# Joining two consecutive gate or up pieces of an expert into one 2 MiB transfer in a fused attention, mLSTM and MoE layer

## The reference, cut to what matters

```python
hg = jnp.einsum('td,edf->tef', xt, w_gate)            # w_gate, w_up: 16 x 2048 x 512
hu = jnp.einsum('td,edf->tef', xt, w_up)
h = jax.nn.silu(hg) * hu * combine[:, :, None]
ff = jnp.einsum('tef,efd->td', h, w_down)             # w_down: 16 x 512 x 2048
ple = (p[l] @ w_ple[l]) * jax.nn.sigmoid(h1 @ w_ple_gate[l])   # w_ple_gate: 2048 x 2048
out = layer_norm(DN_ALPHA * h1 + ff + ple, ln2_g[l], ln2_b[l])
```

## Time and profile before

| | us |
|---|---|
| median of three runs | 1544.24 |
| the profiled execution, its own time | 1543.46 |
| its span, first to last instruction | 1541.9 |
| PE busy in the span | 1482.8 |
| DVE busy | 679.3 |
| ACT busy | 507.1 |
| expert matmuls, gate and up (L896), busy | 227.7 |
| expert matmuls, down (L936), busy | 99.6 |
| PLE gate chunks (L835), busy | 99.0 |

### The profile page before, as it was taken

One profiled execution on the slowest core, in us unless ns is written; L12 is line 12 of the kernel. 1 busy time (PEld: TensorE's weight loads), 2 busy tenths in 40 slices (PEclk: granted clock), 3 DMA queues, 4 the chain that ended last, 5 costly groups with the idle time before them and its releaser, 6 DMA issues.

```text
span 1541.9 us, 16783 instructions
## 1 busy us (share of the span) xinstructions
PE 1482.8 (96%) x6612; PEld 997.9 (65%) x6612; DVE 679.3 (44%) x932; ACT 507.1 (33%) x691; POOL 53.9 (3%) x62
## 2 busy tenths in 40 slices
PE   7999999999999999999999999899998999999893
PEld 6887788888777888888888886533433533343331
DVE  5546665457656555454545655611022121211136
ACT  4444444455544444434444433400200200020011
POOL 0000000043300000000000000000000000000000
PEclk9999999999999999999999999999999999999996
DMA  9554555554444555655555965099999999999994
GB/s 304 184 171 163 164 173 197 176 164 151 149 137 135 167 183 186 203 191 191 190 192 191 364 225 186 9 407 416 389 417 419 419 396 418 419 392 418 419 403 165
DMA packets 132205, 394.88 MB, mean 256 GB/s; under 512 B 13216, under 2 KB 15904, under 8 KB 107552
## 3 DMA queue, kind: packets, MB, share of 16 engines
q1 hardware_dynamic: 123552, 386.56, 67.6%
q10 hardware_dynamic: 8576, 7.28, 1.4%
HBM read 391.71 MB, written 2.10 MB: 255 GB/s over the span
## 4 chain that ended last, share of the span: by engine, by line
PE 61%; issue 37%; DVE 1%; DMA 1%; ACT 0%; SPq 0%; POOLq 0%; DVEq 0%; POOL 0%
PE bank L472 19%; PE bank L473 18%; PE bank L477 18%; PE bank L767 1%; PE bank L499 1%; PE bank L630 1%; PE bank L652 1%; DMA w_ring<-in_w_in_dram 1%; PE bank L564 1%; PE bank L643 0%; PE bank L679 0%; PE bank L678 0%; DVE res L2121 0%; DVE res L2127 0%; PE bank L737 0%
## 5 line engine op out<-in xcount | busy, mean ns | idle before, releaser
L1465 DVE TENSOR_TENSOR w_lo<-w_ring,w_hi 128x1024 fp32r<-128x1024 f32 (+1 forms) x312 | 381.8, 1226 | 307.3 <-ACT w_hi L1062 306.5
L1062 ACT ACTIVATE w_hi<-w_ring 128x1024 fp32r<-128x1024 f32 (+1 forms) x312 | 327.3, 1050 | 317.4 <-PE bank L477 313.7
L472 PE MATMUL bank<-w_hi,xT_hi 128*128 128x512 f32 (+1 forms) x864 | 346.5, 401 | 3.9 <-ACT w_hi L1062 3.9
L473 PE MATMUL bank<-w_hi,xT_lo 128*128 128x512 f32 (+1 forms) x864 | 334.9, 388 | 0.0
L896 PE MATMUL bank<-moe_ring,xg 128*64 128x512 f32 x1024 | 227.7, 595 | 14.3 <-DMA moe_ring<-in_w_up_dram 8.4
L477 PE MATMUL bank<-w_lo,xT_hi 128*128 128x512 f32 (+1 forms) x864 | 229.3, 387 | 0.0
L472 PEld LDWEIGHTS bank<-w_hi,xT_hi 128*128 128x128 f32 x864 | 162.3, 188 | 40.5 <-issue 7.6
L473 PEld LDWEIGHTS bank<-w_hi,xT_lo 128*128 128x128 f32 x864 | 162.5, 188 | 32.4 <-issue 1.9
L477 PEld LDWEIGHTS bank<-w_lo,xT_hi 128*128 128x128 f32 x864 | 161.6, 188 | 33.2
L896 PEld LDWEIGHTS bank<-moe_ring,xg 128*64 128x64 f32 x1024 | 73.9, 137 | 162.1 <-issue 160.7
L936 PE MATMUL bank<-moe_ring,moe_hiddenT 128*64 128x512 f32 x448 | 99.6, 594 | 2.0 <-DMA moe_ring<-in_w_down_dram 2.0
(11 more groups left out here) (272 smaller groups left out, 1343.0 us busy)
## 6 DMA issues: line engine op xcount, KB each, us to landing
w_ring<-in_w_in_dram SPq DMA_DIRECT2D x104, 1024.0 KB, 5.0
moe_ring<-in_w_gate_dram SPq DMA_DIRECT2D x64, 1024.0 KB, 11.9
moe_ring<-in_w_up_dram SPq DMA_DIRECT2D x64, 1024.0 KB, 12.8
moe_ring<-in_w_down_dram SPq DMA_DIRECT2D x64, 1024.0 KB, 12.7
w_ring<-in_w_proj_a_dram SPq DMA_DIRECT2D x16, 1024.0 KB, 5.0
w_ring<-in_w_proj_m_dram SPq DMA_DIRECT2D x16, 1024.0 KB, 5.0
w_ring<-in_w_out_dram SPq DMA_DIRECT2D x16, 1024.0 KB, 5.7
moe_ring<-in_w_ple_gate_dram SPq DMA_DIRECT2D x14, 1024.0 KB, 10.8
```

The costliest lines, as they stand in the source:

```text
L472: mm(b, lh(k, m), WH[:, s, kk, 0:width], start=start and kk == 0, stop=False)
L473: mm(b, ll(k, m), WH[:, s, kk, 0:width], start=False, stop=False)
L1062: fn(WH[:, h % 4, :, 0:width], W32[:, h // 2, 2 * (h % 2):2 * (h % 2) + 2, 0:width], ACT.Copy).then_inc(hi_ready, 1)
L1465: v.tensor_tensor(WL[:, h % 4, :, 0:width], W32[:, h // 2, 2 * (h % 2):2 * (h % 2) + 2, 0:width], WH[:, h % 4, :, 0:width].bitcast(F32), A ...
```

## The change

- The 8 up slots of a pair come in another order: `up_place(i)` gives gate groups 0 and 1, up groups 0 and 1, gate 2 and 3, up 2 and 3.
- The loads of two consecutive slots (always the same matrix) are listed as expert 0 of both, then expert 1 of both. Where their two places adjoin (not places 7 and 0), one transfer of 2 MiB loads both, with rows of 16 KB, and increments the semaphore of the first place alone. `LANDED` says for each piece which semaphore and which value tell that it is there.
- SP waits for such a transfer until both places are free.
- PE adds 4 to `ring_used` after every second up slot, in place of 2 after each.
- PLE chunks 0 and 2 stand behind slot 3 of pairs 0 and 1, not behind slot 2.
- ACT's sigmoid waits for slot 5 in place of slot 6.
- The overflow path (more than 64 tokens for an expert) keeps its single transfers, with its semaphore values adjusted. It does not run with these inputs.

```diff
@@ -62,7 +62,7 @@
-CHUNKS_IN = (("up", 0, 2), ("up", 0, 5), ("up", 1, 2), ("up", 1, 5), ("up", 2, 5), ("down", 1, 1), ("up", 3, 5),
+CHUNKS_IN = (("up", 0, 3), ("up", 0, 5), ("up", 1, 3), ("up", 1, 5), ("up", 2, 5), ("down", 1, 1), ("up", 3, 5),
@@ -74,12 +74,41 @@
     for slot in range(SLOTS_OF[item[0]]):
-        LOADS += [item + (slot, 0), item + (slot, 1)]
+        if item[0] == "down":
+            LOADS += [item + (slot, 0), item + (slot, 1)]
+        elif slot % 2:
+            LOADS += [item + (s, e) for e in range(2) for s in (slot - 1, slot)]
...
+def joint(m):
+
+    return LOADS[m][0] == "up" and LOADS[m][2] % 2 == 0 and m % RING < RING - 1
+
+SIGNALS = [0] * RING
+LANDED = []
+for m in range(N_LOADS):
+    if m and joint(m - 1):
+        LANDED.append(LANDED[-1])
+    else:
+        SIGNALS[m % RING] += 16
+        LANDED.append((m % RING, SIGNALS[m % RING]))
...
+def up_place(i):
+
+    return 2 * (i // 4) + i % 2, i // 2 % 2
@@ -334,23 +363,25 @@
-            def ring_load(m, dst, src):
+            def ring_load(m, dst, src, n=1):
 
+                s, m = m % RING, m + n - 1
                 if m < 4:
                     sp.wait_ge(lo_ready, HALVES * T_END + 2 * m + 2)
                 elif m < RING:
                     sp.wait_ge(slot_free, SLOT_CREDIT + HALVES * T_END)
                 else:
                     sp.wait_ge(ring_used, m - RING + 1)
-                sp.dma_start(dst, src).then_inc(ring_in[m % RING], 16)
+                sp.dma_start(dst, src).then_inc(ring_in[s], 16)
...
-                    ring_load(m, ring_rows(s), up_part(2 * n + e, i))
+                    if joint(m):
+                        ring_load(m, ring_rows(s, 2), up_part(2 * n + e, i, 2), 2)
+                    elif not m or not joint(m - 1):
+                        ring_load(m, ring_rows(s), up_part(2 * n + e, i))
@@ -821,7 +855,7 @@
-                pe.wait_ge(ring_in[m % RING], 16 * (m // RING + 1))
+                pe.wait_ge(ring_in[LANDED[m][0]], LANDED[m][1])
@@ -906,7 +940,9 @@
-                    up_slot(w, i, b, 2 * (n % 2)).then_inc(ring_used, 2)
+                    last = up_slot(w, i, b, 2 * (n % 2))
+                    if i % 2:
+                        last.then_inc(ring_used, 4)
@@ -1377,7 +1413,7 @@
             def sig(n):
-                used("up", n, UP_SLOTS - 2)
+                used("up", n, UP_SLOTS - 3)
```

More of the change, by code:

```diff
@@ L82, with landed_over_at @@
 PAIR_LOADS = 2 * (UP_SLOTS + DOWN_SLOTS)
+def joint(m):
[8 more added lines that the diff above has]
+        LANDED.append((m % RING, SIGNALS[m % RING]))
+def landed_over_at(m):
+    first = N_LOADS + (m - N_LOADS) % RING
+    return SIGNALS[m % RING] + 16 * ((m - first) // RING + 1)
+def up_place(i):
+    return 2 * (i // 4) + i % 2, i // 2 % 2
 def turn_bank(n):
@@ L335, in _, with up_part, ring_rows @@
             down_v = w_down.rearrange("l e (t p) n -> p (l e) t n", p=P)
[L337 to L343, removed]
-            def ring_load(m, dst, src):
+            def up_part(e0, i, n=1):
+                kg, mat = up_place(i)
+                w = up_v if mat else gate_v
+                return w[:, bass.ds(e0, 1), 4 * kg:4 * kg + 4 * n, :].rearrange("p e t f -> p (e t) f")
+            def ring_rows(s, n=1):
+                return RW[:, s:s + n, :].rearrange("p s (t f) -> p (s t) f", t=4)
+            def ring_load(m, dst, src, n=1):
+                s, m = m % RING, m + n - 1
                 if m < 4:
@@ L893, in up_slot @@
                 for t in range(4):
-                    k = 4 * (i // 2) + t
+                    k = 4 * up_place(i)[0] + t
                     for e in range(2):
-                        last = mm(B[b0 + i % 2][CAP * e:CAP * e + CAP, :], xg[:, k, (e0 + e) * CAP:(e0 + e) * CAP + CAP],
+                        last = mm(B[b0 + up_place(i)[1]][CAP * e:CAP * e + CAP, :], xg[:, k, (e0 + e) * CAP:(e0 + e) * CAP + CAP],
                                   w[e][:, t * NC:t * NC + NC], start=k == 0, stop=k == KT - 1)
@@ L1025, in landed_over @@
                                     m = m0 + 2 * i + e
-                                    pe.wait_ge(ring_in[m % RING], 16 * (m // RING + 1) + 16 * (2 * PAIR_LOADS // RING) * g)
+                                    pe.wait_ge(ring_in[m % RING], landed_over_at(m) + 16 * (2 * PAIR_LOADS // RING) * g)
                                 return [RW[:, (m0 + 2 * i + e) % RING, :] for e in range(2)]
```

## The result

| | before | changed |
|---|---|---|
| median, us | 1543.88 (4 runs, 1542.23 to 1544.55) | 1596.45 (4 runs, 1593.37 to 1600.33) |
| ratio, 95% interval | | 1.0343 (1.0328 to 1.0358) |
| profiled execution, span | 1541.9 | 1591.6 (own time 1593.37) |
| mean granted clock | 0.990 | 0.979 |

The change costs 52.6 us, twice the forecast of 26 and beyond the end of the range (1590). The direction and the place are as forecast; the size is not.

A forecast was written before the change was run, and what follows sets the result against it. The prediction took DMA and PE, nearly level over an eight-place ring, as the bound from about 1000 us. It added 25.7 us of PE waits to 1543.46, giving 1569.2, and 0.8 for the median: 1570 us, range 1556 to 1590.

The forecast's parts named there:

- What bounds the kernel: From about 1000 us, DMA (127.6 us per two pairs) and PE (124 us) are within 5%, eight ring places between them.
- The mechanism: Gate and up slots free four places after two slots and need both 2 MiB transfers landed, so PE waits and DMA runs dry.
- the walk: Place-by-place calculation of the expert part from traced durations: PE waits 15.3 us before the change, 41.0 us after.
- The rate of the 16 KB row: Gate and up loads: 2 MiB takes 4.93 us against 5.00, 4 us less transfer in all, bounds 0 and 7.
- carried on place by place: Expert part, transfers in queue order with traced durations: 25.7 us more PE waits than the kernel before.
- price of 2.05 us: SP's ring queue: time from a release of places until bytes flow, taken from the release at 999.8 us.
- slow long rows: 16 KB rows flow much slower, towards the instruction fetches' price: 1610 us at 3.0 us a MiB, beyond 1700 at full price; 5%.
- no difference: Dry spots mostly vanish or are hidden by PE's work, leaving 1552 us or less; 7%, of which 3% within 0.2%.
- a fixed cost for each transfer: Each queued transfer carries a fixed cost that merging halves, making the kernel faster, for example 1540 or 1532 us; 4%.
- The signs: Profile from 1000 us: gate and up waits about 39 us, 375 to 400 GB/s, 2 MiB landing median above 10 us.
- the clock rival: PE's clock falls after eight waits of about 3 us or more in the expert part, losing 23 us: 1593 us; 12%.
- The range: Eight-in-ten range for the whole kernel, 1556 to 1590 us, covering the forecast's own 1562 to 1583 and most of the clock case.

The follow-up runs named there:

- split rows: Changed kernel with each joined 2 MiB transfer issued as two of 1 MiB with 8 KB rows, back to back, same waits: 1598.97 us, ratio 1.0354.
- One place less: Kernel before the change, with SP waiting for one more freed place ahead of each load, as if the ring had 7 places: 1552.09 us, ratio 1.0056.
- the release by four: Kernel before with new slot order and moved PLE chunks, plus 4 places freed after every second up slot; 1 MiB transfers loaded slot by slot: 1554.70 us, ratio 1.0061.
- the expert order: Changed kernel with only the joining switched off: expert 0's two pieces, then expert 1's, 1 MiB each, 4 places freed together: 1567.87 us, ratio 1.0140.
- two places less: Kernel before the change, with SP waiting for two more freed places ahead of each load, as if the ring had 6 places: 1576.79 us, ratio 1.0219.
- the runs with idle matmuls: Changed kernel with identity matmuls on PE ahead of its waits, three amounts: full 1604.40 us, half 1583.52 us, half without those lacking a wait 1586.75 us.

## Why the prediction was wrong

- **What bounds the kernel** was right: the first 996 us did not change, and everything lies in the balance of DMA and PE over the ring.
- **The mechanism** was right: waits at the slots that the walk named, the first at 1016.5 us (forecast: near 1017), the ring's first load at 1002.6 (1003.6), the DMA dry in many small spots.
- **The rate of the 16 KB row** (4 us less of transfer) is not to be seen: joined or split rows gave 1.0343 and 1.0354, whose intervals overlap, though these are too wide to rule 4 us out. But from 1189 to 1196 us, where only 16 KB rows are in the queue, 431 GB/s moved, against 429 for the fastest stretch of 8 KB rows: of the two ends, 0 and 7 us, it lies nearer to 0.
- **The term that failed first** is the step "carried on place by place": +25.7 us of waits, measured +34.8. Its price of 2.05 us was taken where the queue was wholly dry, the flow where it was well filled, and nothing was added for a transfer issued somewhat more than 2 us before the one ahead ends; the passage at 1012 us shows that this is not free. One place less changed little (9 forecast, 8.6 measured). Everywhere else the walk was too low: 4 for 10 with the release by four, 8 for 23 with the expert order, 23 for 33 with two places less, 26 for 52 with the change, the clock's share in them included. In waits alone it is 4 for 6.2, 8 for 13.7, 23 for 25.5 and 25.7 for 34.8. How much of the last is the price of the queue, and how much places freed late by slots at the lower clock, is not told apart.
- **The term that failed second** is the clock. It was put as a rival of 12%, in place of the forecast, where it had to be a term of the sum: the forecast's own waits of 3 to 4.3 us lay beside a row in which a wait of 2.5 us was followed by the lower clock. It measured 14.0 us in the expert matmuls and came on top. Behind eight waits the clock was down, as many as the rival had counted, at 1.75 us each in place of 2.9. The count is partly luck: a wait of 1.96 us is among the eight, one of 3.45 us is not. Another 3.6 us lie in the gather, but the release by four alone has them too, without long waits. The rival's ground for doubt, that part of the loss falls into waits anyway, holds for at most some 5 of these us: 10 to 13 came back in the runs with idle matmuls.
- **The rivals** of slow long rows, of no difference, and of a fixed cost for each transfer found nothing in the runs for them; the last is excluded by the run that merges transfers at an unchanged release (0.9997).
- **The signs.** Of what the profile was to show, the wait ahead of gate and up came out at 48.0 us (forecast 39), the slices behind 1035 us at 345 to 411 GB/s (375 to 400), and the landing of 2 MiB transfers at 12.1 us for gate but 9.8 for up (above 10). The sign of the clock rival, a granted clock under 0.97 in stretches behind 1000 us, was met with 0.91.
- **The range** rested on the forecast or the clock. With the clock's 14.0 us as a term the sum is 1584, inside the range; the 9.1 us of waits by which the walk was too low bring it to 1593, the gather's 3.6 to 1597. Either failure alone would have stayed inside.

## What to carry to other kernels

When two resources are nearly level and a small ring lies between them, count what is waited for, landed and freed as one: here it was this grain, and not the size of the transfer, that decided, and a merged transfer was free where its pieces are used and freed together anyway. Waits that a change adds to PE must be priced twice, for themselves and for the lower clock that may follow: here it followed eight of the twelve waits of about 2 us and more, and took 14 us in all. A walk that is calibrated on a kernel without near-dry passages should be tried on a version that has them before its number is trusted.

## What the runs showed of the hardware

- In the changed kernel waits of 4.00 to 5.64 us were all followed by half the clock (granted 0.52 in 1189 to 1196 us); two slots then took 8.6 to 9.1 us instead of 7.09. Of the waits of 1.96 to 3.45 us some were and some were not. Before, waits of up to 1.34 us left the clock at 1.00.
- 1 MiB and 2 MiB transfers with 8 KB rows moved the same 409 GB/s over 500 us when the queue was kept filled.
- A 2 MiB transfer issued some 2.5 us before the end of the one ahead was followed by 2 us at 262 GB/s.
- Two transfers for 64 partitions each, issued one behind the other, did not overlap into one for 128: 254 GB/s at a DMA share of 0.97.
